# A two-block transformer kernel with its loads, norms and mixer tails reordered, and without its filler products

## The chip, the cores and the metric

The kernel runs on one core of one Trainium2 chip. The metric is the device time of one execution in microseconds (us); lower is better. The core has five engines that run side by side: TensorE (PE, with its weight loads as PEld), VectorE (DVE), ScalarE (ACT), GpSimd (POOL) and SyncE (SP, which here only issues DMAs).

## The reference, cut to what matters

256 tokens of width 1024 in float32 pass through two layers of a first block and one layer of a second block.

```
for l in range(2):
    x = x + 0.5 * swiglu(rms_norm(x), ffn1_w_in[l], ffn1_w_out[l])      # hidden width 2816
    h = rms_norm(x);  uv, c_q, c_kv, k_rope, z, xbc, dt, gates = split(h @ w_in[l])
    y_a = gmlp(uv);  y_b = latent_attention(c_q, c_kv, k_rope);  y_c = state_space(z, xbc, dt)
    merged = sum_b sigmoid(gates_b) * (y_b @ w_branch[l, b])            # 3 branches
    x = x + merged @ w_out[l]
    x = x + 0.5 * swiglu(rms_norm(x), ffn2_w_in[l], ffn2_w_out[l])
h = x
h = h + delta_rule_and_s5_mixer(rms_norm(h)) @ w_out_2
h = h + cross_attention(rms_norm(h), mem_2)
h = h + swiglu(rms_norm(h))
out = rms_norm(h)
```

## The kernel before, in words

All weights stream through a ring of four SBUF slots of up to 1 MB (`ring`); SP issues one DMA per slot and waits, per slot, for a semaphore that says when it is free (`load`, line 160, and `chunk` in `ffn_sync`, line 356). `products_done` counts chunks whose products are made; `landed` counts arrivals. PSUM is used as four banks `acc` for the large products, alternating by the parity of a group number, and four banks `turn` for transposes and small products.

The five feed-forward parts (FFN) and the last part of each mixer use split products: a weight w is parted into w_hi (ACT copies it to the fp32r type, L383 or L213) and w_lo = w - w_hi (DVE, L387 or L217), the activation likewise, and `three` (L221 to L223) adds three fast products. All other products take float32 operands directly and are recorded as two MATMULs each (L189, L203, L253, L416).

An FFN runs as: a first gate in plain float32 (L416), ten and a half blocks of gate and up columns, then eleven chunks of `w_down`. For the last four of these all products of token tile 0 come first, then those of tile 1, so that the addition to x and the norm of tile 0 can run beside tile 1. Between two parts stands a joint: DVE adds the result to x (L536), ACT squares and takes the root (L265, L268), DVE scales (L277 or L295), PE transposes (L314), DVE copies with the gain to xT (L283 or L298). In the `apart` form DVE finishes xT of tile 0 before it adds tile 1.

The mixer of a layer projects in this order on PE: U, V, CQ, gmlp mix, KV, XBC0, transposes of the latents (L940, L945), transposes of the gmlp result (L904), the dt product with 8 columns (L990), XBC1, Z, and so on, then the gates. Its tail (from the sixth gate on) is the split gate, branches 0 and 1, the softmax transposes (`qs_pt_pe`, L1303), attention values (`qs_pv_pe`, L1321), branch 2, transposes of the merged rows (L1376), and the output projection. Each engine's order is written out by hand in `mixer_pe`, `mixer_act` and `mixer_vec`; the engines meet only through semaphores, and an engine waits in order. The parts of the tail's weights lie in two buffers each (`part_hi`, `part_lo`).

`keep_busy` (L303, recorded on L306) issues products of `ident` and `causal` whose result is never read; it stands ahead of most waits of PE: 18 products at the start, 7 or 5 at the norms, 4 at each first gate, 5 before XBC0, 2, 6, 5 and 6 in each mixer tail, 7 in the cross attention, 127 in all.

Of the kernel before, what the change touches and what calls it, by code (L numbers as in the profile page):

```python
# [24 lines left out]
P = 128  # L25
TOK = 256
# [59 lines left out]
def build(nc, t, out):  # L86
    with ExitStack() as ctx:
# [18 lines left out]
        ring = sb("ring", [P, RING, SLOT])  # L106
        x = sb("x", [P, MT, D])
# [71 lines left out]
        def group_pe(pe, G, c, aT, ks, n, n_used=None, for_x=False):  # L179

            k0, K, nu = 0, sum(ks), n_used or n
            for i, kc in enumerate(ks):
                wait_chunk(pe, c + i)
                w = slot(c + i, kc, n)
                for m in range(MT):
                    if i == 0:
                        wait_acc_free(pe, G, m)
                    for k in range(kc):
                        ins = pe.matmul(acc[bank(G, m)][:, 0:nu], aT[:, k0 + k, m * P:(m + 1) * P], w[:, k, 0:nu],  # L189
                                        start=(k0 + k == 0), stop=(k0 + k == K - 1))  # L190
                    if for_x and i == len(ks) - 1 and m == 0:
                        ins.then_inc(tile0_done, 1)
# [4 lines left out]
        def tile_pe(pe, G, c, aT, m):  # L197

            wait_acc_free(pe, G, m)
            for i in range(2):  # L200
# [4 lines left out]
                if m == MT - 1:  # L205
                    ins.then_inc(products_done, 1)

        def part_act(act, s, c, e, hi, k=4, n=512):
# [6 lines left out]
        def part_vec(vec, s, c, e, hi, lo, k=4, n=512):  # L215
            vec.wait_ge(s.hi, e + 1)
            vec.tensor_tensor(lo[:, e % 2], slot(c, k, n), hi[:, e % 2].bitcast(F32), ALU.subtract).then_inc(s.lo, 1)  # L217
# [7 lines left out]
        def split_group_pe(pe, s, G, c, e, a_hi, a_lo, hi, lo, n_chunks, kc=4, for_x=False):  # L225

            for i in range(n_chunks):
                pe.wait_ge(s.lo, e + i + 1)
                for m in range(MT):
                    ms = slice(m * P, (m + 1) * P)  # L230
                    if i == 0:
                        wait_acc_free(pe, G, m)
                    for k in range(kc):
                        ins = three(pe, acc[bank(G, m)][:, :], a_hi[:, i * kc + k, ms], a_lo[:, i * kc + k, ms],
                                    hi[:, (e + i) % 2, k, :], lo[:, (e + i) % 2, k, :],
                                    i == 0 and k == 0, i == n_chunks - 1 and k == kc - 1)
                    if for_x and i == n_chunks - 1 and m == 0:
                        ins.then_inc(tile0_done, 1)
                ins.then_inc(products_done, 1)

        def turned_group_pe(pe, G, c, aT, n_tiles, n, K=KD):
# [5 lines left out]
            for f in range(n_tiles):  # L247
                q = f // 2
                if f % 2 == 0:
# [38 lines left out]
        def add_norm_vec(vec, add, s, gain):  # L288

            for m in range(MT):  # L290
# [5 lines left out]
                for hf in range(2):  # L296
                    vec.wait_ge(s.pe, s.p0 + 2 * m + hf + 1)
                    vec.tensor_tensor(xT[:, 4 * hf:4 * hf + 4, m * P:(m + 1) * P],  # L298
                                      turn[2 * m + hf][:, :].rearrange("p (k n) -> p k n", k=4),
                                      gain.unsqueeze(2).broadcast_to([P, KD, P])[:, 4 * hf:4 * hf + 4, :],  # L300
                                      ALU.mult).then_inc(s.vec, 1)

        def keep_busy(pe, o, n):  # L303

            for _ in range(n):
                pe.matmul(o[:, 0:TOK], ident[:, :], causal[:, :], start=True, stop=True)  # L306

        def norm_pe(pe, s, nb=xn, tiles=(0, 1), busy=0):
            keep_busy(pe, turn[2 * tiles[0]], busy)
# [46 lines left out]
        def ffn_sync(sync, f, c0, w_gate, w_up, w_down, aside=None):  # L356

            def chunk(r, src, i=0):
                sync.wait_ge(products_done, c0 + r + 1)
# [29 lines left out]
        def ffn_pe(pe, f, n, c0, G0, between, asides={}):  # L389
# [17 lines left out]
            def first_gate():  # L407


                wait_acc_free(pe, G0, 0)  # L410
                keep_busy(pe, acc[bank(G0, 0)], 4)
                pe.wait_ge(n.vec, n.v0 + 8)
                wait_chunk(pe, c0)
                for ft in range(2):
# [124 lines left out]
        def add_to_x(vec, c_last, G, factor, use):  # L539

            for m in range(MT):
                add_tile_to_x(vec, m, c_last, G, factor, use)

# [59 lines left out]
        part_hi = over_big("part_hi", 21056, 2, 4, 512)  # L603
        part_lo = over_big("part_lo", 25152, 2, 4, 512)
# [160 lines left out]
        norms_in = [Norm(norms, (20 * l, 32 * l, 12 * l), l < DEPTH, apart=l > 0) for l in range(DEPTH + 1)]  # L765

        def layer_program(l):
# [22 lines left out]
            def params_sync(sync, l):  # L790
                for name, r, k in (("mix_norm", "mix", 8), ("ffn2_norm", "ffn2", 8),
# [15 lines left out]
                            lo=sem(f"part_lo_ready{l}"))  # L807
# [23 lines left out]
            def mixer_sync(sync, l):  # L831
                def w_in(c, name, n, kc=4):
                    for i in range(2):
                        load(sync, c + i, lay("w_in", l)[:, i * 512:(i + 1) * 512, COLS[name]:COLS[name] + n]
                             .rearrange("o (k p) n -> p (o k) n", p=P), 4, n)
# [63 lines left out]
            def gm_turn_pe(pe):  # L899
                pe.wait_ge(cq.vec, 7)  # L900
# [12 lines left out]

            def cq_act(act):
                for i, (G, c, w) in enumerate(((G_CQ, C_CQ, QR), (G_KV, C_KV, KVR))):
                    wait_products(act, c + 1)
                    for m in range(MT):
                        act.activation(junk[:, 0:w], acc[bank(G, m)][:, 0:w], ACT.Square,
                                       accum_out=stat[:, 16 + 2 * i + m:17 + 2 * i + m]).then_inc(cq.act, 1)
                        act.wait_ge(cq.act, 2 * i + m + 1)  # L920
# [2002 lines left out]
```

## Time and profile before

| what | value |
|---|---|
| time, median of 3 runs | 1966.35 us (1964.43 to 1967.27) |
| the profiled execution's own time | 1966.4 us |
| its span | 1964.6 us |
| PE busy | 1913.6 us |
| DVE busy | 932.7 us |
| ACT busy | 709.2 us |
| mean granted clock of TensorE | 0.987 |

The page counts an engine as busy while an instruction of it runs. A matmul's record includes its pipeline, so PE at 97% is occupied and not at its peak, and filler products count as busy.

### The profile page before, as it was taken

The page shows a single profiled execution, that of the slowest core. Times are in us where ns is not written, and L with a number is a line of the kernel's source. Part 1 is how long each engine was busy: PE and PEld are TensorE (multiplying, and loading weights), DVE is VectorE, ACT ScalarE, POOL GpSimd, SP SyncE. Part 2 cuts the span into 40 slices and gives each one's busy share as a digit, 9 for nine tenths or more (in the row PEclk, how much of TensorE's full clock was granted, in tenths as well). Part 3 has the DMA queues.
Part 4 walks back from the last instruction along what each step waited for, and adds up shares of the span by engine and source line. Part 5 has one row for each costly group of instructions (what it writes and reads, how often), then busy time and mean ns, then how long its engine had stood idle before and what let it go on. Part 6 is the DMA issues. An engine that isn't in the chain of part 4 may idle for free.

```text
span 1964.6 us, 25874 instructions
## 1 busy us (share of the span) xinstructions
PE 1913.6 (97%) x10898; PEld 1571.9 (80%) x10898; DVE 932.7 (47%) x1166; ACT 709.2 (36%) x813; POOL 77.9 (4%) x145
## 2 busy tenths in 40 slices
PE   9999999999999999999999999999999999999998
PEld 8998585577999899985855678998787975759996
DVE  4545134467554445441335674545667431134453
ACT  5543213143554345432131343554223111124542
POOL 0000000000000000000000002000371100000000
PEclk9999999999999999999899999999998899999999
DMA  6545434343553565454344337636444213326353
GB/s 236 175 139 192 147 124 153 129 137 120 193 172 127 192 215 171 142 193 143 128 145 133 132 108 138 229 117 211 149 135 115 65 65 128 129 86 215 128 182 128
DMA packets 192246, 293.06 MB, mean 149 GB/s; under 512 B 7218, under 2 KB 126804, under 8 KB 192164
## 3 DMA queue, kind: packets, MB, share of 16 engines
q1 hardware_dynamic: 189908, 287.72, 43.3%
q0 software_dynamic: 1936, 4.14, 2.0%
q8 instruction: 63, 1.03, 0.2%
q14 instruction: 19, 0.16, 0.0%
q10 hardware_dynamic: 320, 0.01, 0.0%
HBM read 289.49 MB, written 2.36 MB: 149 GB/s over the span
## 4 chain that ended last, share of the span: by engine, by line
PE 89%; DVE 6%; DMA 2%; ACT 2%; issue 1%; POOL 0%; DVEq 0%; SPq 0%; ACTq 0%; POOLq 0%
PE acc L221 17%; PE acc L223 17%; PE acc L222 17%; PE acc L189 15%; PE acc L253 7%; PE acc L416 2%; PE acc L2389 1%; PE acc L203 1%; PE acc L2697 1%; DMA ring<-in_ffn_w_out 1%; DMA ring<-in_ffn_w_in 1%; DVE w_lo L387 1%; PE acc L2094 1%; PE acc L1168 1%; PE turn L314 1%
## 5 line engine op out<-in xcount | busy, mean ns | idle before, releaser
L387 DVE TENSOR_TENSOR w_lo<-ring,w_hi 128x2048 fp32r<-128x2048 f32 x160 | 362.8, 2290 | 271.4 <-ACT w_hi L383 271.0
L221 PE MATMUL acc<-xT_hi,w_hi 128*128 128x256 f32 x1680 | 477.4, 284 | 6.9 <-DVE w_lo L387 6.9
L222 PE MATMUL acc<-xT_lo,w_hi 128*128 128x256 f32 x1680 | 476.3, 284 | 0.0
L223 PE MATMUL acc<-xT_hi,w_lo 128*128 128x256 f32 x1680 | 476.2, 283 | 0.0
L383 ACT ACTIVATE w_hi<-ring 128x2048 fp32r<-128x2048 f32 x160 | 302.1, 1913 | 217.2 <-DMA ring<-in_ffn_w_out 110.2
L221 PEld LDWEIGHTS acc<-xT_hi,w_hi 128*128 128x128 f32 x1680 | 323.5, 193 | 7.3 <-issue 7.1
L222 PEld LDWEIGHTS acc<-xT_lo,w_hi 128*128 128x128 f32 x1680 | 323.5, 193 | 0.1
L223 PEld LDWEIGHTS acc<-xT_hi,w_lo 128*128 128x128 f32 x1680 | 323.5, 193 | 0.0
L189 PE MATMUL acc<-ring,xT 128*128 128x512 f32 (+2 forms) x736 | 300.4, 567 | 0.8 <-DVE xT L2677 0.8
L189 PEld LDWEIGHTS acc<-ring,xT 128*128 128x128 f32 x736 | 139.1, 190 | 152.3 <-issue 139.7
L221 PE MATMUL acc<-w_hi,hT_hi 128*128 128x512 f32 x440 | 172.9, 393 | 4.4 <-DVE w_lo L387 4.4
L223 PE MATMUL acc<-w_hi,hT_lo 128*128 128x512 f32 x440 | 171.4, 390 | 0.0
L222 PE MATMUL acc<-w_lo,hT_hi 128*128 128x512 f32 x440 | 171.4, 389 | 0.0
L253 PE MATMUL acc<-xT,ring 128*128 128x256 f32 x640 | 145.9, 391 | 3.1 <-DVE xT L283 1.3
L253 PEld LDWEIGHTS acc<-xT,ring 128*128 128x128 f32 x640 | 125.3, 197 | 22.2 <-issue 1.6
L474 ACT ACTIVATE big<-acc 128x512 f32<-128x512 f32 x55 | 32.8, 597 | 234.3 <-PE acc L223 234.3
L504 DVE TENSOR_TENSOR big<-big,acc 128x512 f32<-128x512 f32 x55 | 37.8, 686 | 159.8 <-ACT big L474 159.7
L221 PEld LDWEIGHTS acc<-w_hi,hT_hi 128*128 128x128 f32 x440 | 82.6, 188 | 25.2 <-issue 6.4
L223 PEld LDWEIGHTS acc<-w_hi,hT_lo 128*128 128x128 f32 x440 | 82.6, 188 | 17.3
L222 PEld LDWEIGHTS acc<-w_lo,hT_hi 128*128 128x128 f32 x440 | 82.7, 188 | 16.4
L217 DVE TENSOR_TENSOR part_lo<-ring,part_hi 128x2048 fp32r<-128x2048 f32 x24 | 54.7, 2287 | 36.0 <-ACT part_hi L213 36.0
L213 ACT ACTIVATE part_hi<-ring 128x2048 fp32r<-128x2048 f32 x24 | 45.9, 1914 | 70.3 <-PE acc L223 69.8
(507 smaller groups left out, 2065.8 us busy)
## 6 DMA issues: line engine op xcount, KB each, us to landing
ring<-in_ffn_w_in SPq DMA_DIRECT2D x88, 1024.0 KB, 5.6
ring<-in_w_in SPq DMA_DIRECT2D x48, 1024.0 KB, 5.0
ring<-in_ffn_w_out SPq DMA_DIRECT2D x44, 1024.0 KB, 4.9
ring<-in_w_branch SPq DMA_DIRECT2D x12, 1024.0 KB, 5.0
ring<-in_w_out SPq DMA_DIRECT2D x12, 1024.0 KB, 5.0
ring<-in_w_gate SPq DMA_DIRECT2D x11, 1024.0 KB, 5.2
ring<-in_w_up SPq DMA_DIRECT2D x11, 1024.0 KB, 6.6
ring<-in_w_down SPq DMA_DIRECT2D x11, 1024.0 KB, 5.0
```

Of the source, the lines that this page charges most:

```text
L189: ins = pe.matmul(acc[bank(G, m)][:, 0:nu], aT[:, k0 + k, m * P:(m + 1) * P], w[:, k, 0:nu], start=(k0 + k == 0), stop=(k0 + k == K - 1))
L213: act.activation(hi[:, e % 2], slot(c, k, n), ACT.Copy).then_inc(s.hi, 1)
L217: vec.tensor_tensor(lo[:, e % 2], slot(c, k, n), hi[:, e % 2].bitcast(F32), ALU.subtract).then_inc(s.lo, 1)
L221: pe.matmul(o, a_hi, wh, start=start, stop=False)
L222: pe.matmul(o, a_hi, wl, start=False, stop=False)
L223: return pe.matmul(o, a_lo, wh, start=False, stop=stop)
L253: ins = pe.matmul(acc[bank(G, q)][:, (f % 2) * TOK:(f % 2) * TOK + TOK], w[:, k % kc, f * P:(f + 1) * P], aT[:, k, :], start=(k == 0), sto ...
L383: act.activation(w_part(w_hi, r), raw_part(c0, r), ACT.Copy).then_inc(f.hi, 1)
L387: vec.tensor_tensor(w_part(w_lo, r), raw_part(c0, r), w_part(w_hi, r).bitcast(F32), ALU.subtract).then_inc(f.lo, 1)
L416: ins = pe.matmul(acc[bank(G0, 0)][:, ft * TOK:(ft + 1) * TOK], raw_part(c0, 0)[:, k, ft * P:(ft + 1) * P], xT[:, k, :], start=(k == 0), s ...
L474: act.activation(gate_s[:, jj % 2], acc[bank(G0 + jj, 0)][:, :].rearrange("p (k n) -> p k n", k=2), ACT.Silu).then_inc(acc_read[bank(G0 + ...
L504: vec.tensor_tensor(h_s[:, jj % 2], gate_s[:, jj % 2], acc[bank(G0 + jj, 1)][:, :].rearrange("p (k n) -> p k n", k=2), ALU.mult).then_inc( ...
```

## The change: what it does

1. **No filler.** `keep_busy` and all its calls go.
2. **Loads by subtraction.** A raw `w_down` chunk is no longer held until its products are made: its slot is free once w_lo is computed (`f.lo`), since the products read w_hi and w_lo. The same holds for the four loads after an FFN (`raw_freed`), in the mixer, in the FFN that follows layer 0 and in the second block.
3. **Tail parts.** `part_hi` has four buffers instead of two, and w_lo is written in place over the raw chunk (`ring_lo`). ACT no longer waits for earlier products there.
4. **Tail reordered.** On PE the order is gate 5, branch 0, softmax transposes, half of branch 1, attention values, the other half, then the last branch by tiles with the transposes of merged tile 0 between, then the output projection by tiles with those of tile 1 between. ACT makes the softmax exponentials ahead of gate 5; DVE's order is rewritten to match.
5. **Latent apart.** ACT and DVE finish the statistics and reads of CQ before those of KV.
6. **dt between.** The two dt products go between the tiles of XBC1, and the gmlp transposes after XBC1.
7. **Norms.** Only the very first norm and the mixer norms are in the `apart` form; the others add and scale both tiles before the four gain copies. Transposes of tile 0 no longer stand inside the pass of tile 1 ahead of layer 1 and of the second block.
8. **Projections by tiles.** The second halves of the two output projections in the second block finish tile 0 first (`tile_pe`).
9. **At the start** ACT takes one square root of a constant while x is on its way, and the gain transpose stands first on PE.

```diff
-        def load(sync, c, src, k, n, turns=0):
-            sync.wait_ge(products_done, c + 1 + RING * turns)
+        def load(sync, c, src, k, n, freed=None):
+            sync.wait_ge(*(freed or (products_done, c + 1)))
...
         def part_act(act, s, c, e, hi, k=4, n=512):
             wait_chunk(act, c)
-            if e >= 2:
-                wait_products(act, c - 2)
-            act.activation(hi[:, e % 2], slot(c, k, n), ACT.Copy).then_inc(s.hi, 1)
+            act.activation(hi[:, e % RING], slot(c, k, n), ACT.Copy).then_inc(s.hi, 1)
...
+        def raw_freed(f, j):
+            return f.lo, RING + N_IN + KF // 2 - RING + j + 1
...
             def chunk(r, src, i=0):
-                sync.wait_ge(products_done, c0 + r + 1)
+                if after and r < RING and type(i) is int:
+                    sync.wait_ge(*raw_freed(after, r))
+                elif r < N_IN:
+                    sync.wait_ge(products_done, c0 + r + 1)
                 sync.wait_ge(f.lo, r + 1 + RING * i)
...
-                keep_busy(pe, acc[bank(G0, 0)], 4)
                 pe.wait_ge(n.vec, n.v0 + 8)
...
+            def dt_pe(pe, m):
+                pe.wait_ge(cq.vec, 6)
+                for k in range(KD):
+                    ins = pe.matmul(turn[m][:, 0:8], xT[:, k, m * P:(m + 1) * P],
...
-                keep_busy(pe, turn[2], 5)
                 turned_group_pe(pe, G_XBC0, C_XBC0, xT, 4, 512)
                 cq_pe(pe)
+                turned_group_pe(pe, G_XBC1, C_XBC1, xT, 4, 520, between=dt_pe)
                 gm_turn_pe(pe)
-                dt_pe(pe)
-                turned_group_pe(pe, G_XBC1, C_XBC1, xT, 4, 520)
...
-                branch_pe(pe, 0)
-                branch_pe(pe, 1)
+                branch_pe(pe, 0, 0)
+                branch_pe(pe, 0, 1)
                 qs_pt_pe(pe)
+                branch_pe(pe, 1, 0)
                 qs_pv_pe(pe)
-                branch_pe(pe, 2)
-                merged_pe(pe)
-                wait_acc_free(pe, G_WO, 0)
-                keep_busy(pe, acc[bank(G_WO, 0)], 6)
-                pe.wait_ge(tail.vec, 8)
+                branch_pe(pe, 1, 1)
+                last_branch_pe(pe)
...
+                tail_part_act(act, 2, 3)
+                qs_act3(act, 0)
+                qs_act3(act, 1)
+                gate_act(act, 5)
                 branch_in_act(act, 1)
-                tail_part_act(act, 2, 3)
-                gate_act(act, 5)
...
+            def last_branch_pe(pe):
+                b = BRANCHES[2]
+                pe.wait_ge(tail.vec, 4)
+                for m in range(MT):
+                    for n in range(2):
+                        ins = split_chunk_pe(pe, tail, G_BR + 4 + n, m, C_BR + 4 + n, 6 + n, yT_hi[:, b], yT_lo[:, b], part_hi)
+                        ins.then_inc(tail.pe if m == 0 else products_done, 1)
+                        if m == 1 and n == 0:
+                            merged_pe(pe, 0)
```

## Rows read from the trace of the kernel before

**Rows 1.** The page: busy time and share of the span, instructions.

```profile
PE 1913.6 (97%) x10898; PEld 1571.9 (80%) x10898; DVE 932.7 (47%) x1166; ACT 709.2 (36%) x813; POOL 77.9 (4%) x145
```

**Rows 2.** PE's groups by line and form: busy us, mean ns, idle before.

```profile
L221 PE MATMUL acc<-xT_hi,w_hi 128*128 128x256 f32 x1680 | 477.4, 284 | 6.9 <-DVE w_lo L387 6.9
L221 PE MATMUL acc<-w_hi,hT_hi 128*128 128x512 f32 x440 | 172.9, 393 | 4.4 <-DVE w_lo L387 4.4
L306 PE MATMUL turn<-causal,ident 128*128 128x256 f32 x176 | 43.8, 401 | 3.0 <-POOL causal L733 2.2 <-DVE big L1311 0.8
L306 PE MATMUL acc<-causal,ident 128*128 128x256 f32 x78 | 18.4, 381 | 0.0
```

**Rows 3.** Stretches: length, PE busy and records, granted clock, DMA share, GB/s.

```profile
281.10:284.50 3.40, 3.40 (x10) 0.50 0.02 5
699.90:706.50 6.60, 5.69 (x32) 1.00 0.64 214
967.20:977.40 10.20, 10.20 (x35) 0.50 0.14 52
1438.20:1441.60 3.40, 1.44 (x12) 1.00 0.97 362
1441.60:1445.00 3.40, 3.40 (x12) 0.50 0.04 11
1496.00:1500.00 4.00, 2.09 (x5) 1.00 1.01 176
```

**Rows 4.** The chain that ended last, in time: start us, us, what.

```profile
2.19 10.90 PE turn L306 x36
17.80 7.17 PE acc L416 x32
250.14 7.78 PE acc L189 x32
260.50 14.05 PE acc L253 x64
277.75 3.48 PE turn L990 x32
281.23 15.60 PE acc L253 x64
966.02 5.47 PE turn L990 x32
971.49 16.90 PE acc L253 x64
```

**Rows 5.** ACT in order of time: start us, us, instruction, idle before.

```profile
13.58 1.91 ACT L383 ACTIVATE w_hi<-ring 128x2048 fp32r<-128x2048 f32 x1 [3.94 <-DMA ring<-in_ffn_w_in]
435.66 1.28 ACT L1285 ACT_TABLE_LOAD   x1
```

**Rows 6.** DVE in order of time, at two joints.

```profile
19.86 2.49 DVE L332 TENSOR_TENSOR xT_lo<-xT,xT_hi 128x512 fp32r<-128x512 f32 x4
704.53 1.29 DVE L298 TENSOR_TENSOR xT<-turn,gain 128x512 f32<-128x512 f32 x2 [0.75 <-PE turn L314]
```

**Rows 7.** PE in order of time, around the latents and in the mixer tail.

```profile
276.66 1.09 PE L904 MATMUL turn<-ident,big 128*128 128x128 f32 x8 [1.01 <-DVE big L952]
450.21 2.78 PE L1303 MATMUL turn<-ident,big 128*128 128x128 f32 x24
...
454.58 2.89 PE L1321 MATMUL turn<-big 128*64 128x128 f32 x48
...
474.70 1.97 PE L1376 MATMUL turn<-ident,xn 128*128 128x128 f32 x16 [0.52 <-DVE xn L1368]
```

**Rows 8.** The chain in the tail, at the first products of branch 2 and of the output projection.

```profile
460.60 0.50 PE acc L221
...
480.34 0.50 PE acc L221
480.84 0.24 PE acc L222
```

More of the change, by code:

```diff
@@ L223, in three, with split_chunk_pe, turned_group_pe @@
             return pe.matmul(o, a_lo, wh, start=False, stop=stop)
[L225 to L241, printed above, removed]
+        def split_chunk_pe(pe, s, G, m, c, e, a_hi, a_lo, hi, first=True, last=True):
+            pe.wait_ge(s.lo, e + 1)
+            if first:
+                wait_acc_free(pe, G, m)
+            ms = slice(m * P, (m + 1) * P)
+            for k in range(4):
+                ins = three(pe, acc[bank(G, m)][:, :], a_hi[:, k, ms], a_lo[:, k, ms], hi[:, e % RING, k, :],
+                            slot_lo(c, 4, 512)[:, k, :], first and k == 0, last and k == 3)
+            return ins
+        def turned_group_pe(pe, G, c, aT, n_tiles, n, K=KD, between=None):
             kc = K // 2 if K == KD else K
@@ L248, in turned_group_pe @@
                 q = f // 2
+                if between and f % 2:
+                    between(pe, f // 2)
                 if f % 2 == 0:
@@ L295, in add_norm_vec, with norm_pe @@
                 vec.tensor_scalar(xn[:, m, :], x[:, m, :], stat[:, 4 + m:5 + m], None, ALU.mult).then_inc(s.vec, 1)
[L296 to L309, printed above, removed]
+                if s.apart:
+                    turned(2 * m)
+                    turned(2 * m + 1)
+            if not s.apart:
+                for b in range(4):
+                    turned(b)
+        def norm_pe(pe, s, nb=xn, tiles=(0, 1)):
             for b in range(2 * tiles[0], 2 * tiles[-1] + 2):
@@ L763, in ffn_views, with layer_program @@
             return part(0), part(FF), lambda i: d[:, 2 * P * i:2 * P * (i + 1), :].rearrange("o (k p) n -> p (o k) n", p=P)
-        norms_in = [Norm(norms, (20 * l, 32 * l, 12 * l), l < DEPTH, apart=l > 0) for l in range(DEPTH + 1)]
-        def layer_program(l):
+        norms_in = [Norm(norms, (20 * l, 32 * l, 12 * l), l < DEPTH, apart=l == 0) for l in range(DEPTH + 1)]
+        def layer_program(l, f_before):
             C_FFN1, G_FFN1 = N_CHUNK_LAYER * l, N_GROUP_LAYER * l
@@ L1004, in sd_cs_pe @@
                 pe.wait_ge(dts.vec, 16)
+                pe.wait_ge(gm.vec, 7)
                 for m in range(MT):
@@ new lines, in branch_pe @@
+                ins.then_inc(products_done, 1)
+            def last_branch_pe(pe):
+                b = BRANCHES[2]
+                pe.wait_ge(tail.vec, 4)
+                for m in range(MT):
+                    for n in range(2):
[3 more added lines that the diff above has]
+                            merged_pe(pe, 0)
@@ new lines, in branch_gate_vec @@
+            def branch_gate_vec(vec, j, n):
+                b = BRANCHES[j]
+                for m in range(MT):
+                    wait_acc_read(vec, G_GATE + 2 * b + n, m)
+                wait_products(vec, C_BR + 2 * j + n)
+                for m in range(MT):
+                    g = bank(G_BR + 2 * j + n, m)
+                    dst = xn[:, m, n * 512:(n + 1) * 512] if j == 0 else br_t[:, n, m, :]
+                    vec.tensor_tensor(dst, acc[g][:, :], gates[:, m, b * D + n * 512:b * D + (n + 1) * 512],
+                                      ALU.mult).then_inc(acc_read[g], 1)
@@ L1375, in merged_pe @@
+            def merged_pe(pe, m):
+                pe.wait_ge(br.vec, 6 + 2 * m)
+                for hf in range(2):
+                    b = 2 * m + hf
                     for k in range(4):
@@ L2723, in fill @@
                     product(pe, *which)
-            norm_pe(pe, nm, tiles=(1,), busy=7)
+            norm_pe(pe, nm)
             pe.wait_ge(nm.vec, nm.v0 + NORM_DONE)
@@ L2856, in second_vec @@
                                          op0=ALU.mult, op1=ALU.mult).then_inc(nf.vec, 1)
-        layers = [layer_program(l) for l in range(DEPTH)]
+        layers = []
+        for l in range(DEPTH):
+            layers.append(layer_program(l, layers[-1][4] if l else None))
+        f_last = layers[-1][4]
         with nc.Block() as block:
```

273 lines of the change are left out of this document (141 added, 132 removed).

## The prediction

> **What bounds the kernel now.** I read the page first: PE is occupied 97% of the span, DVE 47%, ACT 36% [rows 1]. So the end is set by what PE does and by what it waits for, and an edit counts only if it shortens one of them. Next the groups by line and form. Two wait for DVE's w_lo: the down products 4.4 us in all and the block products 6.9 us [rows 2]. The second is one wait, in the last layer's second FFN, where weights land late; no edit touches its cause, small DMAs that POOL issues at that norm. The fillers are 176 + 78 records, 127 products, 62.2 us busy [rows 2]. They hide the real waits: PE looks busy while it has nothing to do. So I read PE in order of time and took the fillers for idle; what lies between the last useful product before a filler and the first after it is the real wait [rows 4, 7, 8]. Last the granted clock by stretch: TensorE stood at half speed, 1.2 of 2.4 GHz, from 281.1 to 284.5, 967.2 to 977.4 and 1441.6 to 1445.0 among others, and at full speed through joints full of fillers [rows 3].
>
> So there are two accounts: waits and slow stretches that the reordering removes, and the clock, which the fillers held up and which nothing will hold any more. The sum starts from the profiled execution's own 1966.4 us (span 1964.6 and 1.8 around it); the median of the runs is the same within 0.1 us.
>
> **Part by part, gains.**
>
> *Start.* Before, 36 filler records run from 2.19 to 13.09, the first gate from 17.80 to 24.97 [rows 4]. After, the preloaded root function and the missing fillers let xT finish near 12. What then binds: chunk 1 of the weights is copied from 13.58 to 15.49 [rows 5], its w_lo follows, some 2.3, then DVE's xT_lo, 2.49 [rows 6], so 20.3 is the earliest the split block can start. The gate runs partly at half clock from about 12.3 and ends near 21.5. Bounds 0 and 4.7 (24.97 - 20.3); I take 3.0, nearer to the floor, since both chains are known.
>
> *Loads by subtraction.* The idle ahead of the down products, 4.4 [rows 2], arises where the last chunk is loaded only after older products, then copied and subtracted. With the slot free at w_lo the load is done long before, and only copy and subtraction (1.9 + 2.3) remain behind the product that frees w_hi, against three chunks of tile 0 products on PE. I take 4.4 (0 to 4.4). The earlier mixer loads gain nothing: PE enters U without a wait. On SP the memory load of the second block moves behind an explicit wait for the same event as before.
>
> *Latent apart.* KV ends at 257.92, XBC0 starts at 260.50 [rows 4]: PE waits for a bank that DVE frees only after KV's statistics. Read right behind CQ it is free about 5 us ahead. 2.6 in each of two layers: 5.2.
>
> *dt between.* L904 waited 1.01 for DVE [rows 7]; behind XBC1 it waits for nothing: 2.0 in two layers. The 32 dt records took 3.48 in layer 0 and 5.47 in layer 1, and XBC1 behind them 15.60 and 16.90 against 14.05 for the equal XBC0 [rows 4]. Both times the clock had fallen right there [rows 3], in or after the stream of products of 8 columns. Halved and set between tiles of full products they should no longer bring it down: 1.55 + 2.85 + 1.99 = 6.4 (0 to 6.4; I take all, the rows being of the same place).
>
> *Tail.* Real waits before, in layer 0: from the end of the softmax transposes (452.99) to L1321 at 454.58, 1.6; from 457.47 to 460.60, 3.1; after branch 2 (48 products of 0.235 from 460.60, so to 471.9) until L1376 at 474.70, 2.8; from 476.67 to 480.34, 3.7 [rows 7, 8]. Together 11.1. In the new order the last three have products beside them. But the transposes now come 11 us earlier, and I laid the engines' new orders side by side with the durations of before. ACT: exponentials from about 421.8 (table load 1.28 [rows 5], then 8 short and 8 longer ones) to 430, a second table load for gate 5, then the input of branch 1 at 433.6, on which DVE sits in order. DVE then: w_lo, gate, second softmax scaling to 441.5, w_lo, gate, and the first copy of a transpose at 445.6. PE reaches the transposes at 439.0, waits to 441.5 and again from 442.5 to 445.7: 5.0 instead of 1.6. Another 0.6 is late at the merged transposes of tile 0, which DVE's w_lo and adds hold up. So 11.1 - 5.6 = 5.5 gained a layer, 11.0 in two (bounds: 22 if no new wait, 0 if the new ones are as long as the old).
>
> *Fillers that overran and transposes moved.* At the joint before layer 1 the last copy of xT ended at 705.82 [rows 6] but the gate began at 706.50. Such overrun goes: 0.3 at two joints. There and ahead of the second block 1.0 us of transposes moves from the FFN's last pass into the joint's idle; the copies, no longer `apart`, cost about 0.6 back. With the overrun I take 1.0 and 0.4. Sum 2.0. The other norms end as before, since tile 1's chain is unchanged, and projections by tiles bring only tile 0's part forward, which was never last: 0, hidden behind tile 1's.
>
> Gains: 3.0 + 4.4 + 5.2 + 2.0 + 6.4 + 11.0 + 2.0 = 34.0.
>
> **Part by part, losses.** No time of PE is saved by the fillers as such. What they did shows in the clock: from 699.9 to 706.5, with them, full speed [rows 3]. Without them this joint is a wait of some 4, one short burst of transposes, and over 1 more of waiting. The nearest unfilled case: from 1438.2 to 1441.6 PE was busy 1.44 of 3.40, and then the clock was 0.50 for 3.4 us. On the other side 1496 to 1500, busy 2.09 of 4.00, kept full speed [rows 3]. The joints without filler lie below both, so I let each fall. Price of one fall: from 0 to 4.84 (layer 1's XBC1 and dt together); XBC1 alone lost 1.55 and 2.85, mean 2.2, and this I take, because work after a joint is dense like it. Places: the joints at 503, 700, 1402, 1676 and 1761, the cross attention near 1720, and the new wait in both tails: 8 x 2.2 = 17.6. The joint at 1195 falls too, but the late weights behind it (6.9 of waiting) cover it: 0; were that cover gone, 2.2.
>
> Sum: 1966.4 - 34.0 + 17.6 = 1950.0 us.
>
> The Trainium skill says of the same gate (TensorE: Matmul & The Clock Gate, section Why this matters for your kernels) that long idle gaps between bursts of matmuls send the clock back to half. By it every joint falls, 17.6 in my sum; without it the sum would be 1932.4. The row at 1441.6 agrees; the one at 1496 shows that not every wait does it. This rule speaks against taking the fillers out at all.
>
> **Rivals.**
>
> *The clock holds (7%).* If transposes and short waits suffice, the losses are nil: 1932. For: 1496 to 1500 kept full speed. Against: 1438.
>
> *Every fall costs what layer 1 paid (6%).* The mechanism: the clock, once down in a joint, stays down through the first gate, as in the 10.2 us from 967.2, and each of the eight places costs 4.84, 38.7 in all: 1966.4 - 34.0 + 38.7 = 1971, slower. It decides from 34.0 / 8 = 4.25 a place. Against: in that case dt's 8-column products went on; behind a joint dense work follows, and at 1445 the clock was back after 3.4 us.
>
> *The tail's new waits eat its gain (13%).* DVE is one queue in which branch 1's input, the softmax scaling and w_lo stand in line; if PE waits 10 instead of 5.6 there the tail gains 1 a layer: 1950.0 + 9 = 1959. For: DVE sits about 5 us on ACT in my layout. Against: parts now run four ahead instead of two.
>
> *The dt products still bring the clock down (10%).* In two short streams instead of one, but hardly any columns in either: 6.4 is not gained, 1956.
>
> *The fillers' removal and the waits cancel (4%).* Several sizes off together, 1963 to 1970.
>
> **How the numbers follow.** The forecast, 1943 to 1957, has 60%. This kernel's measurement can tell 0.2%, 3.9 us, from no change: faster means under 1962.5, slower over 1970.3. Faster: 0.60 + 0.07 + 0.10 + most of 0.13 = 0.87; slower the second rival, 0.06; the rest 0.07. The range to hold 8 in 10 leaves out the clock that holds and the slower rival: 1940 to 1962.
>
> **What would show it.** Right: no wait ahead of XBC0 and of the down products; XBC1 with dt inside at about 17.4; the output projection ending some 5 earlier after the sixth gate than before; the granted clock 0.50 for some us at each named joint, the first gates there 9 instead of 7. Wrong: joints at full clock (then faster than said); waits in the tail above 6 a layer, or slow stretches longer than 7 us behind joints (then slower). The idle of the block products should shrink below 6.9, since a slowed gate fills it.

## The result, and the profile after

| | before | changed |
|---|---|---|
| time, median of the runs | 1965.39 us (1962.49 to 1967.27, 4 runs) | 1949.07 us (1946.24 to 1951.6, 4 runs) |
| the profiled execution's time, its span | 1966.4, 1964.6 us | 1946.2, 1944.4 us |
| mean granted clock of TensorE | 0.987 | 0.978 |

The ratio is 0.9918, 95% interval 0.9899 to 0.9937: 16 us faster (12 to 20), where 1950.0 was forecast. In a later set of runs the same kernel gave 0.9935 (0.9916 to 0.9953). Executions in the chip's second, slower state (one of that set took 2121 us) are left out of every ratio in this document.

The page of the changed kernel, its busy row, answers to [rows 1]. PE is busy 43.0 us less. The unread products were 62.2 us of records in [rows 2]; the rest of the difference comes mostly from products that now run at half clock.

```profile
PE 1870.6 (96%) x10644; PEld 1534.0 (79%) x10644; DVE 933.5 (48%) x1168; ACT 708.6 (36%) x815; POOL 77.9 (4%) x145
```

PE's groups by line and form (busy us, mean ns | idle before), against [rows 2]: the down products wait for nothing, the block products 5.3 instead of 6.9. What the unread products had covered now stands in the open, above all the wait of the norms' transposes (L313).

```profile
L224 PE MATMUL acc<-xT_hi,w_hi 128*128 128x256 f32 x1680 | 477.7, 284 | 5.3 <-DVE w_lo L393 5.3
L224 PE MATMUL acc<-w_hi,hT_hi 128*128 128x512 f32 x440 | 172.3, 392 | 0.0
L313 PE MATMUL turn<-ident,xn 128*128 128x128 f32 x144 | 22.1, 303 | 22.6 <-DVE xn L300 22.6
```

PE of the changed kernel in order of time at the start (against [rows 4], where the gate took 7.17), at the first joint, and at the softmax transposes of the first tail (against [rows 7]): start us, us, what, idle before it.

```profile
7.39 1.97 PE L313 MATMUL turn<-ident,xn 128*128 128x128 f32 x8 [2.01 <-DVE xn L300]
11.00 1.97 PE L313 MATMUL turn<-ident,xn 128*128 128x128 f32 x8 [1.64 <-DVE xn L300]
13.76 10.11 PE L421 MATMUL acc<-xT,ring 128*128 128x256 f32 x32 [0.78 <-DVE xT L292]
...
431.07 1.04 PE L1306 MATMUL turn<-ident,big 128*128 128x128 f32 x8
433.48 1.09 PE L1306 MATMUL turn<-ident,big 128*128 128x128 f32 x8 [1.38 <-DVE big L1296]
437.57 1.94 PE L1306 MATMUL turn<-ident,big 128*128 128x128 f32 x8 [3.00 <-DVE big L1314]
...
491.23 1.04 PE L313 MATMUL turn<-ident,xn 128*128 128x128 f32 x8
495.33 1.09 PE L313 MATMUL turn<-ident,xn 128*128 128x128 f32 x8 [3.06 <-DVE xn L300]
497.72 8.79 PE L421 MATMUL acc<-xT,ring 128*128 128x256 f32 x32 [1.30 <-DVE xT L292]
```

The waits of the tail and of the joint are followed by half clock: 8 transposes take 1.04 us at 431 and 1.94 at 437, and the 32 products of the gate take 8.79 us, where before they took 7.07 at the joint. At the start, where the clock has not yet risen, they take 10.11 us against 7.17. The records of that gate show when it rose: 13 products take 5.92 us, the 18 behind them 4.19 (two windows of the same view).

```profile
13.76 5.92 PE L421 MATMUL acc<-xT,ring 128*128 128x256 f32 x13 [0.78 <-DVE xT L292]
19.46 4.19 PE L421 MATMUL acc<-xT,ring 128*128 128x256 f32 x18
```

Stretches of the changed kernel (length, busy and records of PE, PEld, DVE, ACT and POOL, granted clock, DMA share, GB/s), the first in answer to the fall at 281 us in [rows 3]:

```profile
270.00:288.00 18.00, 18.00 (x104) 16.30 (x103) 9.96 (x36) 3.80 (x6) 0.00 (x0) 1.00 0.32 111
436.20:443.00 6.80, 5.43 (x17) 4.69 (x18) 6.41 (x9) 0.00 (x0) 0.00 (x0) 0.50 0.01 2
688.00:706.00 18.00, 13.95 (x67) 11.78 (x66) 13.23 (x15) 11.77 (x12) 0.00 (x0) 0.81 0.04 9
```

In the chain (start us, us, what), against [rows 4]: the conv projection starts as the second latent's product ends, and the second one, dt inside it, runs from 270.71 to 288.10 without the clock falling.

```profile
253.87 1.94 PE acc L193 x8
255.81 13.81 PE acc L253 x64
...
270.71 3.46 PE acc L253 x16
274.17 1.68 PE turn L992 x16
275.85 7.01 PE acc L253 x32
...
284.54 3.56 PE acc L253 x16
```

Where the 20.3 us between the two profiled spans come from, each stretch of PE's work by its length before less its length after (plus is a gain):

| stretch | layer 0 | layer 1 | last part |
|---|---|---|---|
| up to the first split block | +1.1 | | |
| first FFN | +1.0 | +0.7 | |
| to the first conv projection | +2.8 | +2.8 | |
| both conv projections, dt, turns | +3.0 | +6.3 | |
| split gate to end of output projection | +3.6 | +3.9 | |
| joint and first gate | -1.4 | -1.4 | |
| second FFN (layer 1: with the late weights) | +2.3 | +3.3 | |
| joint behind it | -2.3 | -0.4 | |
| second mixer | | | +1.4 |
| joint and query projection; cross attention | | | -2.9; -2.3 |
| last joint; last FFN | | | -2.5; +1.4 |

Two rows need care. Ahead of layer 1 and of the second block, 1.0 us of transposes moved from the FFN into the joint, so the FFN's row shows 1.0 too much gain and the joint's row as much loss. The -0.4 in layer 1 is that joint alone: the 128 products behind it took 30.62 us instead of 27.90, and these 2.7 us are inside the second mixer's +1.4.

### The profile page after: what moved, and what is told of

It reads as the page before. It is cut to its first block, busy times and chain, and to the rows that moved or that the text cites. A ratio compares the mean times of both kernels' runs of the same rounds, so it can differ in the third digit from the quotient of the medians.

```text
span 1944.4 us, 25305 instructions
## 1 busy us (share of the span) xinstructions
PE 1870.6 (96%) x10644; PEld 1534.0 (79%) x10644; DVE 933.5 (48%) x1168; ACT 708.6 (36%) x815; POOL 77.9 (4%) x145
## 4 chain that ended last, share of the span: by engine, by line
PE 89%; DVE 5%; ACT 3%; DMA 1%; issue 1%; DVEq 0%; ACTq 0%; SPq 0%
PE acc L224 17%; PE acc L225 16%; PE acc L226 16%; PE acc L193 15%; PE acc L253 7%; PE acc L205 2%; PE acc L421 2%; PE acc L2425 1%; PE acc L2733 1%; DMA ring<-in_ffn_w_in 1%; DVE xT L292 1%; PE acc L1171 1%; ACT big L1288 1%; ACT part_hi L215 1%; PE acc L2128 1%
## 5 line engine op out<-in xcount | busy, mean ns | idle before, releaser
L193 PE MATMUL acc<-ring,xT 128*128 128x512 f32 (+2 forms) x672 | 275.3, 569 | 0.8 <-DVE xT L2713 0.8
L193 PEld LDWEIGHTS acc<-ring,xT 128*128 128x128 f32 x672 | 127.7, 192 | 138.3 <-issue 125.8
L253 PE MATMUL acc<-xT,ring 128*128 128x256 f32 x640 | 146.3, 390 | 2.6 <-DVE xT L292 2.6
L253 PEld LDWEIGHTS acc<-xT,ring 128*128 128x128 f32 x640 | 124.8, 196 | 20.8 <-DVE xT L292 3.1
L265 ACT ACTIVATE xn<-x 128x1024 f32<-128x1024 f32 x20 | 21.1, 1057 | 153.9 <-DVE x L541 152.9
L541 DVE SCALAR_TENSOR_TENSOR x<-acc,x 128x512 f32<-128x512 f32 x36 | 23.2, 686 | 86.3 <-PE acc L226 60.3
```

The costliest lines, as they stand in the source:

```text
L253: ins = pe.matmul(acc[bank(G, q)][:, (f % 2) * TOK:(f % 2) * TOK + TOK], w[:, k % kc, f * P:(f + 1) * P], aT[:, k, :], start=(k == 0), sto ...
L541: vec.scalar_tensor_tensor(out=xs, in0=acc[bank(G + hf, m)][:, :], scalar=factor, in1=xs, op0=ALU.mult, op1=ALU.add).then_inc(acc_read[ban ...
```

## The experiments

Theory, as predicted: the reordering gains some 34 us and the missing products cost some 18 through the clock. Rival: the products never helped, and their absence is itself a gain. Times are told by their ratio to the kernel before on the same chip; 0.001 is 2 us. The changed kernel stands at 0.9918 and 0.9935, and a difference from it is given as the range between the two. Code is cut to the lines that matter, and some of it is put in words.

**The products put back where the changed kernel waits.**

```
 for b in range(4): m, hf = b // 2, b % 2
+    if b == 2: keep_busy(pe, turn[2], 6)          # joints; 2 ahead of each first gate,
                                                   # 5 and 2 in the cross attention, 3 and 6 in the tails
```

The products ahead of a gate write into the gate's own bank, so the wait for that bank now stands ahead of them.

> The changed kernel with products whose result nobody reads put back only where its own trace shows TensorE waiting: 6 between the transposes of the two tiles at the joints (3.06 us of wait each), 2 ahead of each first gate (1.30 us), 5 and 2 in the cross attention, 3 and 6 between the transposes of the attention weights (waits of 1.38 and 3.00 us). Theory (the stretches at clock 0.50 that follow these waits are the price of having taken the products out): about ten stretches of 3.4 to 6.8 us at half clock, some 1.3 to 2.2 us each, go, and the first gates take 7.1 us again instead of 8.7 to 9.7; the time is 1933 to 1938, 12 to 16 below the changed kernel. Rival (the products give nothing back, because the clock falls for another reason or because they end late and push the real work): 1946 to 1952.

Ratio 0.983 (0.9813 to 0.9848), 1928.67 us: 17 to 21 us less than the changed kernel, more than the theory asked. PE at the first joint:

```profile
487.71 2.75 PE L311 MATMUL turn<-causal,ident 128*128 128x256 f32 x12
490.94 1.09 PE L320 MATMUL turn<-ident,xn 128*128 128x128 f32 x8 [0.47 <-DVE xn L300]
491.87 1.03 PE L311 MATMUL acc<-causal,ident 128*128 128x256 f32 x4
493.33 7.17 PE L429 MATMUL acc<-xT,ring 128*128 128x256 f32 x32 [0.43 <-DVE xT L292]
```

At this joint the products end before the values arrive (0.47 and 0.43 us are still waited), and the gate takes 7.17 us: nothing is pushed, the clock is held. Five stretches at half clock are left of thirteen, 42 us in all; the two profiles of the changed kernel have 87 and 94 us.

**The kernel before without them.** `keep_busy` returns at once; nothing else.

> The kernel before with its unread products taken out and nothing else. Theory (by the changed kernel's thirteen stretches at half clock against six before): eight to ten new stretches at half clock of 1.3 to 2.9 us each, so 12 to 22 us more than before, 1978 to 1988, less at most 3 us that the products themselves cost where they ended late. Rival (the unread products were in the way rather than useful, and their removal is where the gain of the whole change comes from): 1950 to 1962.

Ratio 1.0109 (1.0091 to 1.0126), 1982.46 us: 21 us slower than before, within the theory; its granted clock is 0.972. Three of its stretches, in the tail and at two joints:

```profile
478.00:488.20 10.20, 6.97 (x21) 5.44 (x20) 6.76 (x9) 2.46 (x4) 0.00 (x0) 0.50 0.05 20
512.10:518.90 6.80, 5.93 (x17) 4.60 (x16) 6.80 (x10) 6.77 (x8) 0.00 (x0) 0.50 0.01 2
710.10:716.90 6.80, 5.20 (x16) 4.21 (x17) 5.43 (x7) 6.47 (x7) 0.00 (x0) 0.50 0.18 65
```

So the rival is out, and the two accounts can be read apart: taking the products out costs 21 us in the old order, putting some back gains 17 to 21 in the new one, and the rest of the change gains 1.0109 - 0.9918 or 0.9935, 34 to 37 us.

**VectorE's order in the tail.**

```
 qs_vec5(vec, 0)
+qs_vec5(vec, 1)
 branch_in_vec(vec, 1); tail_part_vec(vec, 4); branch_gate_vec(vec, 0, 0)
-qs_vec5(vec, 1)
+qs_vec6(vec)
 tail_part_vec(vec, 5); branch_gate_vec(vec, 0, 1)
-qs_vec6(vec)
 tail_part_vec(vec, 6)
```

> The changed kernel with one edit on VectorE: both scalings of the attention weights stand ahead of the split of the second branch's input, and the six copies of the turned weights ahead of the last projection parts. Theory (the waits of 1.38 and 3.00 us between the transposes are VectorE's order, and the fall of the clock at 436 to 443 us is theirs): both waits go, 4.4 us, and with them that stretch, 2.2 us or so, in each of two layers: 9 to 13 us less, 1936 to 1940. Rival (the waits only move to the second branch's product, whose inputs VectorE now makes later): within 2 us of the changed kernel.

Ratio 0.9875 (0.9857 to 0.9892), 1936.07 us: 8 to 12 us less, about what the theory said (9 to 13). The transposes of the attention weights wait for nothing; only those of the merged rows still do, 0.8 us a layer:

```profile
L1306 PE MATMUL turn<-ident,big 128*128 128x128 f32 x48 | 5.6, 272 | 0.0
```

**The old order of the tail**, without unread products.

```
-branch_pe(pe, 0, 0); branch_pe(pe, 0, 1); qs_pt_pe(pe); branch_pe(pe, 1, 0)
-qs_pv_pe(pe); branch_pe(pe, 1, 1); last_branch_pe(pe)    # merges inside
+branches 0 and 1; qs_pt_pe(pe); qs_pv_pe(pe); branch 2       # in words
+pe.wait_ge(br.vec, 8); merged_pe(pe, 0); merged_pe(pe, 1)
+output projection with both tiles in each chunk; old orders on ScalarE and VectorE
```

> The changed kernel with the last part of the mixers in the order of the kernel before (branch by branch on TensorE, the merge after the whole third branch, the old orders on ScalarE and VectorE), without unread products. Theory (the new order's gain is the waits it takes away: 11.1 us a layer before against 4.8 us in the changed kernel's trace): the two tails take 6 to 8 us more each, less or more 2 us for a stretch at half clock, so 11 to 16 us more than the changed kernel: 1955 to 1961. Rival (the tail's gain was only the absence of late unread products, not the order): within 3 us of the changed kernel.

Ratio 1.0034 (1.0021 to 1.0046): 19 to 23 us more than the changed kernel, beyond the theory. PE in its first tail and at the joint behind it:

```profile
445.92 2.89 PE L1322 MATMUL turn<-big 128*64 128x128 f32 x48 [1.59 <-DVE big L1314]
451.94 0.64 PE L224 MATMUL acc<-part_hi,yT_hi 128*128 128x512 f32 x1 [3.13 <-DVE yT_lo L1441]
467.53 1.97 PE L1403 MATMUL turn<-ident,xn 128*128 128x128 f32 x16 [2.68 <-DVE xn L1382]
473.17 0.80 PE L224 MATMUL acc<-part_hi,xT_hi 128*128 128x512 f32 x1 [3.67 <-DVE xT_rest L1451]
499.35 1.46 PE L313 MATMUL turn<-ident,xn 128*128 128x128 f32 x8 [2.46 <-DVE xn L300]
503.11 1.97 PE L313 MATMUL turn<-ident,xn 128*128 128x128 f32 x8 [2.30 <-DVE xn L300]
505.86 9.29 PE L421 MATMUL acc<-xT,ring 128*128 128x256 f32 x32 [0.78 <-DVE xT L292]
```

The waits inside the tail are 11.07 us, the 11.1 that the prediction had read through the unread products, against 4.83 in the changed kernel. The joint adds 1.2 us of waits and a longer slow stretch. But this is not a price of the old tail, for this kernel keeps the changed norm: VectorE scales tile 0 before it adds tile 1 (`add_norm_vec`), and in between it waits 2.89 us for ScalarE's root. That order suits a projection that ends tile 0 early, and not the old one. In the kernel before, VectorE adds both tiles first. From the last product of the projection to the gate it takes 6.60 us before, 6.38 and 6.74 (layer 0 and 1) in the kernel before without products, 6.33 changed, and 8.97 and 8.94 here. The old tail up to its last product takes 88.8 and 88.9 us here, against 82.7 and 82.4 in the changed kernel; this is the price of the tail alone, 12.7 us in the two, and inside the theory's range. The stretch from the split gate to the next split block, in all kernels (us, layer 0 and 1):

| | with unread products | without |
|---|---|---|
| old order | 99.54, 99.62 (before) | 104.58, 104.79 (before, bare) |
| old order in the changed kernel | | 106.67, 106.86 |
| the change's order | 93.40, 93.40 (in the tail too) | 97.41, 97.06 |
| VectorE's order mended too | 88.87, 88.94 (joint and gate alone) | 90.34, 91.98 |

**Both dt products ahead of the conv projection** instead of between its tiles: `dt_pe(pe, 0)` and `dt_pe(pe, 1)` stand ahead of `turned_group_pe` for XBC1, which loses `between=dt_pe`.

> The changed kernel with both short dt products ahead of the second conv projection instead of between its tiles. Theory (in a row they are long enough to bring the clock down, as at 281 us in the kernel before; between the tiles they are not): they themselves cost the same, a stretch of 3.4 us or more at clock 0.50 comes back in each layer, and with it 2 to 4 us in the two together, while VectorE has the dt values earlier, which nobody near waits for: 1948 to 1950 by a difference of +2 to +5. Rival (the fall at 281 us came from the wait of 1.01 us ahead of the turned values, not from the dt products): no difference, within 1 us.

Ratio 0.9964 (0.9951 to 0.9977), 6 to 9 us more where the theory had 2 to 5. The fall is back at the same place in both layers, with no wait over 0.44 us ahead of it:

```profile
268.50:273.90 5.40, 4.96 (x44) 4.75 (x43) 4.89 (x14) 2.37 (x3) 0.00 (x0) 1.00 0.99 349
273.90:277.30 3.40, 3.40 (x9) 2.66 (x10) 3.17 (x12) 0.13 (x1) 0.00 (x0) 0.50 0.13 49
956.60:960.00 3.40, 3.40 (x10) 2.69 (x9) 3.05 (x13) 0.41 (x2) 0.00 (x0) 0.50 0.01 5
```

From the first conv projection to the next group it takes 35.54 and 35.53 us, against 33.17 in both layers of the changed kernel: 4.7 together. The rest of the difference is not explained by this place. The executions of this kernel lie between 1947.7 and 1960.9 us with clocks of 0.977 to 0.970, and the profiled one is the fastest of them; that the others lost more in their other slow stretches fits this, but no trace shows it.

**The latents read together.** `vec.wait_ge(cq.act, 3 * i + 3)` becomes `vec.wait_ge(cq.act, 6)`.

> The changed kernel with VectorE's work on the first latent held back until ScalarE has the statistics of both. Theory (the banks of the first latent come free late, and the first conv projection waits for them, 2.6 us in each layer as in the kernel before): 5 to 6 us more, and if the clock falls behind the wait as well, 7 to 10 us more: 1951 to 1957. Rival (the projection finds its bank free in any case): no difference.

Ratio 0.9967 (0.9956 to 0.9979), 6 to 10 us more. This is the theory's second case. In its chain the projection starts at 256.90 behind VectorE, 2.35 us after the second latent's product; the same in layer 1, and there 3.4 us at half clock behind it.

```profile
256.13 0.63 DVE big L932
256.76 0.14 issue
256.90 14.05 PE acc L253 x64
```

**The loads by subtraction alone**, in the kernel before (the FFN's part shown; the mixers' and the second block's first four loads likewise).

```
-sync.wait_ge(products_done, c0 + r + 1)
+if after and r < RING and type(i) is int: sync.wait_ge(*raw_freed(after, r))
+elif r < N_IN: sync.wait_ge(products_done, c0 + r + 1)
```

> The kernel before with one part of the change alone: the first four loads behind each feed-forward wait for VectorE's subtraction that frees the slot and no longer for TensorE's product, and the down loads likewise. Theory (4.4 us of waits for weights inside the down products go): 4 to 5 us less than before, 1956 to 1961 by a ratio of 0.9975 to 0.998. Rival (that gain is given back at the joint, where VectorE's own order decides): within 1 us of before.

Ratio 0.998 (0.9968 to 0.9993), 3.9 us less (1.4 to 6.3), as the theory said. The down products wait for nothing, and the five passes are 0.6 to 1.4 us shorter each, 5.7 in all.

```profile
L221 PE MATMUL acc<-w_hi,hT_hi 128*128 128x512 f32 x440 | 172.6, 392 | 0.0
```

**The small loads.** First moved: `pool.wait_ge(before, 12)` instead of `1`.

> The changed kernel with GpSimd's small loads for the last part (some hundred KB in small pieces) issued after the eleventh weight split of the second layer's last feed-forward instead of after the first. Theory (they stand in the way of the big weight loads at the joint, and the wait of 5.33 us ahead of the first split block at 1203 us is theirs): that wait goes, and the time is 4 to 6 us lower, 1943 to 1945. Rival (the big loads are late there in any case, or the small ones now hold up a later block by as much): within 1 us.

Ratio 0.9914 (0.9894 to 0.9935): no difference that can be told, so the theory's 4 to 6 us are not shown. The wait at the joint is gone, but a block waits 2.39 us until 1268, so the rival holds in part. Then changed in form, in the joined kernel (below):

```
-for g in range(2):
-    pool.dma_start(s5w[64 * g:64 * g + 64, 0, :], log_dt.rearrange("o (k g) -> g (o k)", g=2)[g:g + 1, :]...)
+pool.dma_start(ldt_pairs, log_dt.broadcast_to([P, 2 * NS]))
```

> The joined kernel (unread products at the joints, first gates and cross attention; the tail's new order), but with GpSimd's small loads back at their old place, behind the first weight split of the second layer's last feed-forward, and one of them changed in form: the 32 step sizes are loaded as one contiguous row for all partitions, 128 bytes each, instead of by two loads that gather every second value in pieces of 4 bytes; ScalarE picks the values out as it reads them. Theory (the two loads in 4-byte pieces alone are what keeps the DMA engines 90 to 99% busy at 0 to 2 GB/s for some 11 us, behind which the weights of the joint come late): that plateau is gone, the weights land within some 11 us of their issue, the wait ahead of the split block is under 1 us, and the ratio is 0.970 to 0.974, at or below the joined kernel's. Rival (the other small loads, in pieces of 64 bytes, hold the engines as long): the wait of 5 to 7 us ahead of the split block is back and the ratio is 0.976 to 0.979.

Ratio 0.9735 (0.9722 to 0.9748), 1908.17 us. The DMA view of the changed kernel from 1170 to 1215 us: busy tenths and GB/s in slices of 1.1 us, the queues' shares, and the median us from issue to landing.

```profile
DMA  9999719990004499990002589899999999899999
GB/s 380 370 364 387 246 28 2 2 1 0 0 0 0 0 0 1 1 1 0 0 13 23 73 103 189 247 315 361 383 384 389 354 382 385 315 290 363 369 378 385
q0 software_dynamic: 608, 0.60, 43.2%
ring<-in_ffn_w_in SPq DMA_DIRECT2D x7, 1024.0 KB, 11.3
wsT<-in_s_log_dt POOLq DMA_DIRECT2D x2, 4.0 KB, 16.1
vecs<-in_norm_x_g POOLq DMA_DIRECT2D x1, 4.0 KB, 18.5
```

From 1176.9 to 1193.0 us alone, GpSimd's queue moved next to nothing and held all engines:

```profile
q0 software_dynamic: 50, 0.01, 99.0%
```

The same of the last kernel, from 1150 to 1205 us, and its block products from the groups by form:

```profile
q0 software_dynamic: 576, 0.60, 7.8%
ring<-in_ffn_w_in SPq DMA_DIRECT2D x11, 1024.0 KB, 6.2
wsT<-in_s_log_dt POOLq DMA_DIRECT2D x1, 16.0 KB, 2.5
vecs<-in_norm_x_g POOLq DMA_DIRECT2D x1, 4.0 KB, 2.0
...
L224 PE MATMUL acc<-xT_hi,w_hi 128*128 128x256 f32 x1680 | 476.3, 284 | 0.0
```

Nearly the same bytes hold the engines 43.2% of 45 us (19 us) or 7.8% of 55 us (4.3 us). No block waits any more, though the loads stand at their old place, where the changed kernel waited 5.33 us and the one with products put back 7.20. So it was the form of the two loads and not their bytes that held the weights up; loads of the old form also stop hurting this joint when they are moved, but then they hurt elsewhere.

**The changed kernel again**, and **three edits joined**: the products at the joints, gates and cross attention; VectorE's order; the small loads one by one, in their old form, each behind the next weight split (`pool.wait_ge(before, next(split))`). Then with **products at the start** as well.

> The changed kernel as it is, beside the next two on one chip, so that their differences are taken from one set of runs and its own spread is seen. It should stand at the ratio of its first runs, 0.990 to 0.994 of the kernel before, with runs some 6 to 12 us apart where the stretches at half clock begin earlier or later in the same work.

> Three edits on the changed kernel: unread products in the waits of the joints, the first gates and the cross attention (not in the mixers' last part), VectorE's order in the mixers' last part as in the experiment on the tail, and GpSimd's small loads one by one behind the weight splits of the first ten blocks. Theory (the three gains lie in different places and add): 12 us for the clock at the joints and in the cross attention, 8 for the tail, 5 for the wait of 5.3 to 7.2 us ahead of the split block at 1203 us: a ratio of 0.975 to 0.980. Rival (the small loads hold up blocks one by one, and the tail's next wait appears): 0.982 or more.

> The same with unread products in the waits at the start too (6 ahead of the first gains, 4 ahead of the first tile, 5 between the tiles, 3 ahead of the first gate). Theory (the first gate's 10.11 us at half clock in the changed kernel are what the start's gain of 3.0 us foundered on): the gate takes 7 to 8 us instead of 10.1, and the time is 2 to 3 us below the kernel without them. Rival (VectorE's split of the input, ready at 20.15 us, ends last instead): no gain, within 1 us.

Ratios 0.9935 (0.9916 to 0.9953), 0.9738 (0.972 to 0.9757) and 0.976 (0.9736 to 0.9783). The changed kernel repeats. The joined one takes 1911.82 us, 35 to 39 us below it, more than the 25 that the theory had added up; by themselves products and order had gained 17 to 21 and 8 to 12, and moved small loads nothing that can be told. The start gave nothing that can be told either. PE at the start of the last of them:

```profile
14.82 7.07 PE L430 MATMUL acc<-xT,ring 128*128 128x256 f32 x32
21.54 0.47 PE L224 MATMUL acc<-xT_hi,w_hi 128*128 128x256 f32 x1
```

The gate runs at full clock, but starts 0.86 us later than without them (14.82 against 13.96): the first unread products, at half clock, run until 7.68, where the gain transpose had begun at 5.27, and those behind them end late too. The split block starts 0.68 us earlier (21.54 against 22.22). Later the profiled execution waited 3.64 us for weights until 1200, against 1.41 without products at the start, and 6.49 us until 1430, against 0.80, for values that come through DRAM by GpSimd's transfers. So the two ratios don't price the start.

The lowest median is that of the joined kernel with whole rows, 1908.17 us against 1959.87 of the kernel before on that chip; the changed kernel would stand at 1944 to 1947 there, an estimate from its two ratios. Its ratio of 0.9735 can't be told from the 0.9738 of the joined kernel with the small loads one by one, so whole rows saved the waits and the spreading, and no time beyond it.

## Why the prediction was right

The forecast was 1950.0 and its two accounts hold. The gains of 34.0 measured 34 to 37 (the changed kernel against the one before without its unread products), the losses of 17.6 measured 17 to 21. The sums match better than their terms, and part of the match is luck. No run takes back the start, the buffers of the tail's parts, the norms' form or the second block's projections by tiles alone; for these there is the trace only. Step by step:

*Loads by subtraction, 4.4:* right; 3.9 by the ratio, 5.7 by the passes.

*Latent apart, 5.2:* right; taking it back costs 4.7 of waits, and 6 to 10 in all.

*dt between, 8.4 with its wait:* the two stretches gained 3.0 and 6.3 us, XBC1 with dt took 17.55 where 17.4 was said, and the clock held. That the 8-column products in a row are what brings it down is shown by the experiment that joins them. The size was partly luck, though. The order of the kernel before stands in three traces, and in layer 1 its clock fell there for 10.2 us [rows 3], for 6.8 without unread products and for 3.4 with the new loads; the stretch took 39.46, 37.78 and 36.16 us. The prediction had priced the longest of the three. What the edit itself is worth is the 4.7 of the experiment, and the two waits of 1.01 beside it.

*Tail, 5.5 a layer before its fall:* the new waits are 1.38 + 3.00 + 0.45 = 4.8 where 5.6 was said, at the places named and for the reasons named: VectorE's queue, with the scaling and the first copy behind the input of branch 1. The 5.0 for the first two is a slip of the prediction: with the first 8 transposes (1.04 us) taken out, its own marks give 1.5 + 3.2 = 4.7, and 4.4 was measured. Net of the fall the stretch gained 3.6 and 3.9, said was 3.3, though the sign named in the prediction was "some 5 earlier", which leaves the fall out. The rival of larger waits did not come. What the prediction missed is that these waits were avoidable: ScalarE had the second exponentials at 422, while VectorE stood idle until 425.7 for the input of branch 1; in the mended order they are gone.

*Projections by tiles, 0:* right. From the end of the mixer's output projection to the gate it takes 6.60 us before and 6.33 changed, and at the joint at 1676, between the second block's mixer and its cross attention, it is 6.33 in both kernels. At the last joint it is 7.43 against 6.59 before, since the clock had fallen ahead of the transposes of tile 1. The longer joint of the experiment with the old tail comes with the pairing of the old projection and the changed norm.

*Start, 3.0:* mis-sized; 1.1 here, and 2.0 in the second profile of the same kernel (split block at 23.52 and 22.61, before at 24.62). Two steps of the term were off. The gate began at 13.76 instead of 12.3, since the transposes ahead of it run at half clock too (1.97 us for each 8). And its clock rose later than thought: 9.2 us were said for the gate, 10.11 were measured, with full clock only from 19.7 on. So it ended at 23.87 and not at 21.5. VectorE's chain, said to be ready at 20.3, was ready at 20.15 and was not the limit.

*Losses, eight places of 2.2:* all eight fell, and the joint at 1195 too. The products behind each fall show its price by their own lengths: the gates or projections behind the joints at 503, 700, 1402, 1676 and 1761 took 1.7, 2.6, 2.7, 2.9 and 1.7 us longer than before, the cross attention 2.3, and the work of the two tails, waits left out, 2.8 and 2.6 longer than in the experiment whose tail did not fall. That is 19.3 in all, 2.4 a place. The joint at 1195 lost 1.4, and the block idle behind it shrank from 6.9 to 5.3, as the cover argument had it.

*Not in the sum:* the second mixer took 1.4 us less than before in this profile, although the slowed products at its beginning cost it 2.7, and 2.2 us more than before in the second profile of the same kernel (238.74 and 242.36 against 240.17). Its long stretch at half clock lasted 23.9 us before, and 13.7 and 20.5 in the two. No step of the prediction has this; as far as it helped, it was luck.

The rule of the Trainium skill named in the prediction (TensorE: Matmul & The Clock Gate, section Why this matters for your kernels) agrees with the traces at the joints: the wait of 3.06 us between two bursts of transposes went with half clock at all five joints that have it. It doesn't cover every row here: the dt products in a row lost the clock with no wait over 0.44 us, and one wait of 2.35 us was followed by half clock in layer 1 and not in layer 0.

## What to carry to other kernels

Two edits that act on one wait can't be priced one after the other: a product that nobody reads buys no time of its own engine, yet here such products kept the clock up at the joints, for 17 to 21 us in all, and it hid real waits that looked like work. First take such products out and read the waits; then mend the order; then put products back only into waits that are left, and see that they end before the data come. A stall on a large load may be the fault of a tiny transfer in front of it: look at the bytes per second beside the DMA engines' busy share.

## What the runs showed of the hardware that was not expected

Two loads of 4 KB in pieces of 4 bytes (2 x 64 partitions x 16 values, 2048 pieces) kept the DMA queue of GpSimd busy for some 15 us more than one load of 16 KB in pieces of 128 bytes, and the transfers behind them, the 1 MB loads too, landed late (11.3 against 6.2 us, small ones 16 to 18 against 2 to 4 us). The trace has the two loads as 32 packets of 256 bytes, 64 pieces each, which took 8.0 us apiece on average (15.9 us of all 16 engines); the one load that replaced them is 16 packets of 1024 bytes, 0.25 us apiece. The Trainium skill (DMA: Bandwidth & Descriptors, section Bandwidth) calls transfers under 64 KB dominated by their descriptors and gives some 10.5 ns a packet at its small end. By that the 2048 pieces, each counted as a packet, would be 21.5 us, an estimate; the measured 15.9 is of this size.

Executions of one kernel differ by up to 13 us (1947.7 to 1960.9) with the granted clock between 0.977 and 0.970, while the order of work is the same. Two profiles of the changed kernel show one way: in the second mixer the clock fell at 1494.3 for 13.7 us in one, and at 1489.2 for 20.5 us in the other. The 3.3 us by which the dt stretch gained more in layer 1 than in layer 0 look like the same, by the three traces of the old order.

A projection of 64 products (L253) that begins behind a wait of 2.35 us took 14.05 us in layer 0 and 15.73 in layer 1, one and the same code; only in the second did the clock fall.
